# Moving the SBUF places of the matmul operands by 192 and 224 bytes in a two-block transformer kernel

## The reference

```python
def swiglu(h, w_in, w_out):                       # w_in 1024 x 5632, w_out 2816 x 1024
    g, u = jnp.split(h @ w_in, 2, axis=-1)
    return (jax.nn.silu(g) * u) @ w_out

# first block, per layer; x_lat and x_ctx are two streams of 256 tokens
x = layer_norm(ALPHA * x + 0.5 * gate * swiglu(modulate(x, shift, scale), w_in, w_out), g, b)
x = layer_norm(ALPHA * x + gate * mixer(modulate(x, shift, scale)), g, b)   # gmlp (1024 -> 6144 -> 1024) or attention
x = layer_norm(ALPHA * x + 0.5 * gate * swiglu(...), g, b)

# second block, per layer; one stream
x = x + 0.5 * gt1 * swiglu(modulate(rmsnorm(x), sh1, sc1), w_in, w_out)
x = x + gt2 * (concat(moba_attention, conformer_conv, gla) @ mix_w_out)     # from h @ mix_w_in, 1024 x 3088
x = x + 0.5 * gt3 * swiglu(modulate(rmsnorm(x), sh3, sc3), w_in, w_out)
```

## Time and profile before

| | |
|---|---|
| median of three runs | 3104.11 us |
| profiled execution, its own time | 3106.1 us |
| its span, first to last instruction | 3104.4 us |
| TensorE clock granted | 0.993 |
| TensorE busy with matmuls | 3043.4 us, 98% |
| weight loads (beside the matmuls) | 2732.1 us, 88% |
| VectorE, ScalarE, GpSimd busy | 2027.8, 969.3, 679.8 us |
| chain that ended last | PE 89%, DVE 6%, ACT 3% |

### The profile page before, as it was taken

The page is one execution under the profiler, slowest core; times in us unless marked ns, Lnnn a source line. Parts: engine busy times, 40 slices in busy tenths (PEclk is TensorE's granted clock), DMA queues, the critical chain, the costliest instruction groups (busy, mean ns, idle before and its releaser), DMA issues.

```text
span 3104.4 us, 46661 instructions
## 1 busy us (share of the span) xinstructions
PE 3043.4 (98%) x19308; PEld 2732.1 (88%) x19308; DVE 2027.8 (65%) x2134; ACT 969.3 (31%) x1027; POOL 679.8 (22%) x614
## 2 busy tenths in 40 slices
PE   8999999999999999999998899999999999999999
PEld 5888889988888888888887699899989999999999
DVE  4854368766288533784637766676797757669764
ACT  2111232212132121311215333333544333354443
POOL 1210100124013010130101022231462313228110
PEclk9999999999999999999999999999999999999999
DMA  7543335332235332453523387586547768755564
GB/s 264 191 153 94 104 108 184 117 104 81 100 124 203 109 95 95 148 185 112 203 88 122 122 263 239 182 272 217 199 157 251 256 200 275 235 188 193 162 189 150
DMA packets 501668, 522.79 MB, mean 168 GB/s; under 512 B 15732, under 2 KB 433830, under 8 KB 501478
## 3 DMA queue, kind: packets, MB, share of 16 engines
q1 hardware_dynamic: 498536, 513.76, 50.1%
q0 software_dynamic: 2944, 6.32, 1.0%
HBM read 518.97 MB, written 1.05 MB: 168 GB/s over the span
## 4 chain that ended last, share of the span: by engine, by line
PE 89%; DVE 6%; ACT 3%; issue 1%; DMA 1%; POOL 0%; SPq 0%; DVEq 0%; ACTq 0%
PE ps L2243 30%; PE ps L2418 16%; PE ps L2329 15%; PE ps L2271 8%; PE ps L2442 8%; PE ps L2308 2%; DVE wl L1246 2%; PE ps L2287 1%; PE ps L2355 1%; ACT wh L837 1%; PE ps L2688 1%; PE ps L2132 1%; PE ps L2548 1%; DVE acc L1219 1%; PE ps L2720 1%
## 5 line engine op out<-in xcount | busy, mean ns | idle before, releaser
L1246 DVE TENSOR_TENSOR wl<-wraw,wh 128x2048 fp32r<-128x2048 f32 x341 | 831.8, 2439 | 554.8 <-ACT wh L837 550.1
L837 ACT ACTIVATE wh<-wraw 128x2048 fp32r<-128x2048 f32 x341 | 652.5, 1914 | 917.2 <-PE ps L2329 374.5
L2243 PE MATMUL ps<-xh,wh 128*128 128x512 f32 (+1 forms) x1504 | 560.3, 373 | 0.4 <-DVE xl L1298 0.3
L2243 PE MATMUL ps<-xh,wl 128*128 128x512 f32 (+1 forms) x1504 | 548.4, 365 | 0.0
L2243 PE MATMUL ps<-xl,wh 128*128 128x512 f32 (+1 forms) x1504 | 548.3, 365 | 0.0
L2418 PE MATMUL ps<-xh,wh 128*128 128x258 f32 x1408 | 404.7, 287 | 4.3 <-DVE xl L1449 3.3
L677 POOL CAST hh<-ht 128x256 f32 (+1 forms) x176 | 140.3, 797 | 1194.5 <-DVE ht L1633 861.0
L2418 PE MATMUL ps<-xh,wl 128*128 128x258 f32 x1408 | 400.6, 284 | 0.0
L2418 PE MATMUL ps<-xl,wh 128*128 128x258 f32 x1408 | 399.8, 284 | 0.0
L1219 DVE SCALAR_TENSOR_TENSOR acc<-mraw,svec,acc 128x1024 f32<-128x1024 f32 x259 | 344.4, 1349 | 5.7 <-DVE prea L1285 0.4
L2243 PEld LDWEIGHTS ps<-xl,wh 128*128 128x128 f32 x1504 | 283.8, 189 | 45.7
(11 more groups left out here) (438 smaller groups left out, 5496.4 us busy)
## 6 DMA issues: line engine op xcount, KB each, us to landing
wraw<-in_ffn_w_in SPq DMA_DIRECT2D x352, 512.0 KB, 4.8
wraw<-in_ffn_w_out SPq DMA_DIRECT2D x176, 512.0 KB, 4.1
mraw<-in_ada_w SPq DMA_DIRECT2D x72, 1024.0 KB, 6.0
mraw<-in_w_mod SPq DMA_DIRECT2D x64, 1024.0 KB, 6.3
wraw<-in_gmlp_w_in SPq DMA_DIRECT2D x48, 512.0 KB, 4.2
wraw<-in_mix_w_in SPq DMA_DIRECT2D x48, 512.0 KB, 4.6
wraw<-in_gmlp_w_out SPq DMA_DIRECT2D x24, 512.0 KB, 3.8
first_w<-in_w_mod SPq DMA_DIRECT2D x8, 1024.0 KB, 10.9
```

Source lines behind the costliest of these rows:

```text
L837: act.activation(wh[:, slot], wraw[:, slot], ACT.Copy).then_inc(whi_done, 1)
L1246: dve.tensor_tensor(wl[:, slot], wraw[:, slot], wh[:, slot].bitcast(F32), ALU.subtract)\
L2243: m = pe.matmul(ps[:, bank, 0:width], a, b, start=k == p == 0, stop=k == KD - 1 and p == 2)
```

## The change

Three small tensors change places. `mhalf` (128 bytes for each partition) and `negm` (64 bytes) now stand right ahead of the place of the inputs, and `gm_rstd` (16 bytes, which takes 32 of room) between it and the place of the hidden units. The inputs' halves and all that shares their place move up by 192 bytes, the hidden units and all that shares theirs by 224 bytes: `xh` begins at 141504, `xl` at 157888, `xl2` at 150208, `hh` at 174304, `hl` at 198880. Most small tensors behind the hidden place move by 64 to 192 bytes; the last ones stay. `wraw`, `wh`, `wl`, `gm_lo`, `acc` and `x` stay at multiples of 2048. On each engine the same instructions stand in the same order with the same sizes; their addresses alone differ.

```diff
@@ -219,6 +219,8 @@
             with ExitStack() as a:
                 return [a.enter_context(nc.sbuf_tensor(n, s, d)) for n, s, d in shapes]
 
+        mhalf = sb("mhalf", [P, TT * 16])
+        negm = sb("negm", [P, 16])
         xh, xl = alias(("xh", [P, KD, 2 * T], F32R), ("xl", [P, KD, 2 * T], F32R))
@@ -237,6 +239,7 @@
         sb("place_of_inputs", [P, 2 * KD * 2 * T])
 
+        gm_rstd = sb("gm_rstd", [P, 2 * TT])
         hh, hl = alias(("hh", [P, 12 * 512], F32R), ("hl", [P, 12 * 512], F32R))
@@ -270,15 +273,12 @@
         sb("place_of_hidden", [P, 2 * 12 * 512])
         gm_st = sb("gm_st", [P, 2 * TT, GM_UNITS, 6])
-        gm_rstd = sb("gm_rstd", [P, 2 * TT])
         gm_col = sb("gm_col", [P, 2, 2 * GM_UNITS])
@@
         scrap = sb("scrap", [P, TT])
-        mhalf = sb("mhalf", [P, TT * 16])
         nrm = sb("nrm", [P, TT, 16])
-        negm = sb("negm", [P, 16])
         den = sb("den", [P, 2, 16])
```

## The result

The change made the kernel slower: 3130.57 us, the median of four runs (3125.17 to 3136.84), against 3102.79 us (3101.14 to 3104.64) of the kernel before on the same chip. The ratio is 1.0085, 95% interval 1.0072 to 1.0097. The forecast was 3080 us with a range of 3022 to 3113, so it was wrong in its sign. The profiled execution took 3125.17 us, 19.1 us over that of before (3106.1).

The account below looks back on a forecast made before the run. TensorE's start-to-start distances were taken to bound the kernel; 11,112 matmuls x 2.2 ns = 24.5 us off the profiled 3106.1 gave 3081.6, stated as 3080 us because that execution lies 2.0 us over the median; range 3022 to 3113.

Parts of the forecast that it names:

- What bounds the kernel: TensorE, busy 98% of the span: time is the sum of its start-to-start distances, with some 60 us of real gaps.
- VectorE, ScalarE, GpSimd and the DMAs at zero: Reads, writes and the first_w landing at moved places: zero taken, with 3 us and 0.5 us named as possible costs.
- the 13.3 ns: Time per full-pace float32r matmul beyond its columns, 226.7 against 213.3 ns at 512 columns, 120.0 against 106.7 at 256.
- One price of -2.2 ns for all 11,112 matmuls: Streamed and loaded inputs and hidden units leaving the aligned arrangement: each matmul 2.2 ns shorter, 24.5 us less in all.
- upper loss: The 0.13 us step, 8 to 10 ns over, for all moved matmuls: some 90 to 110 us more.
- The 256-column lines: L2271, L2442 and the 256-column matmuls of L2243 and L2287: 2.2 ns less each, as for 512 columns.
- The count of L2271: Loaded inputs, 192 over, against streamed weights at 0: 3 x 832 = 2,496 matmuls leave the aligned arrangement.
- L2418 stays at 119.7: Second block's inputs, offsets already spread over eight chunks: same mean of 119.7 ns, zero change.
- C: Rival: one more collision, 6.7 ns on hidden units (L2329, L2442), inputs give nothing; 25 us more, 3129 us; chance 0.19.
- 33 us for the streamed inputs: Rival C's side case: the same extra step on the 4,944 streamed-input matmuls alone would cost 33 us.
- A: Rival: both offsets miss the collisions, every matmul at the short step; 74 us less, 3030 us, or 2976; chance 0.24.
- B: Rival: the extra is the same at any common offset, 226.7 and 120.0 ns as before; 3104 us; chance 0.16.

Follow-up runs that it names:

- e4: Weights, inputs and hidden units all moved by 192 bytes against the kernel before, each distance kept: 3106.73 us, 1.0001 times before.
- e1: Computation left out, 61 bare stretches of float32r matmuls by width, role and places: 512 columns 226.7 ns at 0, 233.3 at 192; 256 columns 120.0 and 113.3.
- e7: Hidden units moved by 256 bytes against the kernel before, inputs not moved: 3104.14 us, 1.0002 times before.
- e5: Computation left out, 89 bare stretches varying width, places, load width and type: with a load of 64, 512 columns at 0 took 230.0 ns.
- e10b: Computation left out, 31 stretches each entered eight times behind a matmul of another width: 256 columns at 192 took 113.3 ns three times, 117.8 five times.

## Why the prediction was wrong

*What bounds the kernel.* Right: the time is the sum of TensorE's start-to-start distances, and the change shows there or nowhere. VectorE, ScalarE, GpSimd and the DMAs at zero: right (the page after, and e4).

*That addresses set part of the 13.3 ns, with 256 bytes as the distance that matters.* Right, and shown by e1, e4 and e7. The Trainium skill's rule of independent read ports (page "SBUF — State Buffer", section "Who interferes with whom"), weighed in the prediction, would have given no change. The measurement decides: e4 keeps the distances and moves the places, at a ratio of 1.0001; the change moves the distances, at 1.0085.

*One price of -2.2 ns for all 11,112 matmuls.* This is the step that failed. It was read from L2720, 256 columns, mixed offsets, and laid on 5,016 matmuls of 512 columns, of which the trace of before had none off the aligned distance. These cost +6.7 ns, not -2.2: 20.5 and 10.0 us on L2243 and L2329 alone, where 7.6 and 3.4 us less were summed; with the `gm_h` and L2308 stretches, which the sum left out, +35. The bound did not help either: the prediction waved its upper loss off as seen nowhere in the trace, though no row of 512 columns bore on it. It did name this step as the one that would fail if each line had its own price.

*The 256-column lines.* Sign right, size near: L2243 -4.0, L2442 -3.4, L2287 -2.7, L2271 -1.0, together -11.1 us against 13.4 at 2.2 ns each; the rows named as signs, 354 of L2271 at 41.7 us and 258 of L2442 at 30.5, came out to the digit (117.8 and 118.3 ns). The count of L2271 was wrong. Of its 2,496 matmuls 1,056 belong to the mixer of the second block, where the loaded chunks are those of `xh2` and `xl2`, 1088 bytes apart, so they never stood at the aligned distance; what is said of L2271 ahead of the prediction holds for the other 1,440. Those went from 178.8 to 176.1 us. The 1,056 went from 133.2 to 134.9, with 16 of them in a spell of the lower clock after and none before, an estimated 1.4 us.

*L2418 stays at 119.7.* Right: 456 in 54.60 us, 54.59 before.

*The rivals.* C was right in its kind, one more step of 6.7 ns. That its 3129 us is near the 3130.57 is luck, since its place was wrong: it put the step on all the hidden units and cleared the inputs, while it is all the 512-column lines that pay, at 192 and at 224, and L2442 on the hidden units gained. Its last sentence, 33 us for the streamed inputs, had the right lines, but counted 1,488 matmuls of 256 columns with the 3,456 of 512 (which alone make 23). A fell with e1 and e5: 512 columns were never under 226.7 ns at any of the places tried. B fell with the trace after and e1, where common offsets change the pace.

*What stays open.* The mechanism: neither the meetings of the two reads nor a beat of starts alone explains what a narrower load or 504 columns do. Why 112 has one pace and 192 two. Why a load at 144 over stays at 120.0. The four runs of the changed kernel are 12 us apart, and their mean granted clock goes with it: 3125.17 us at 0.995 (the profiled one), 3130.05 and 3131.08 at 0.993, 3136.84 at 0.991. At 0.993, the clock of the profiled execution before (3106.1 us), they are 24 and 25 us over it, which is the +25 of the table. That other entries into the two paces add to the spread is not excluded, since only one trace of the kernel is kept.

## What to carry to other kernels

When a price is read from a trace, read it for each shape that will pay it; a row of 256 columns says nothing on 512, here not even the sign. Before moving operands, time the few pairs of width and distance as bare stretches, and enter each stretch several times: one clean entry hid a second pace that ate more than half of the gain. For float32r matmuls on this chip keep streamed and loaded operands at equal remainders modulo 256 bytes where 512 columns are streamed; 112 over paid where exactly 256 are, and in the bare stretches 8 bytes to either side gained nothing. When two profiled executions differ by a few us, compare their granted clocks before explaining the difference.

## What the runs showed of the hardware

- Of a float32r matmul with a load of 128 columns, start to start, the time depends on the distance between streamed and loaded address, with multiples of 256 bytes all alike: 226.7 to 236.7 ns at 512 columns and 113.3 to 126.7 ns at 256 columns in e1 and e5 (the dearest, in e5, at 4 bytes for 512 columns and at 8 bytes for 256), and up to 130.0 at 104 bytes in e10b. bfloat16 (215.9, 109.2; places 0, 64, 128 and 192) and plain float32 (429.2 for each of two records; 0 and 192) show none of it.
- A pace can have two stable values for one and the same loop, 113.3 and 117.8 ns at a distance of 192. It is taken at the entry and holds for hundreds of matmuls; what picks it is not known.
- 512 columns of float32r never took less than 226.7 ns, and 256 never less than 113.3, at any place tried.
- At the lower granted level, 1.2 GHz, float32r matmuls start 213 ns apart with 256 columns and 427 with 512, against 120.0 and 226.7 at the higher one: there the columns alone set the step (the profiles before and after).
